# Adding the experts' rows to their tokens for two experts at a time, on one Trainium2 core

## The reference, cut to what matters

```python
combine = jnp.sum(jax.nn.one_hot(eid, N_EXPERTS, dtype=jnp.float32) * (g1 * g2)[..., None], axis=1)
acc = jnp.zeros_like(t)
for e in range(N_EXPERTS):
    hid = jax.nn.silu(t @ w_gate[e].astype(t.dtype)) * (t @ w_up[e].astype(t.dtype))
    acc = acc + combine[:, e:e + 1] * (hid @ w_down[e].astype(t.dtype))
```

## Time and profile before

| | us |
|---|---|
| median of 3 runs | 864.66 (863.48 to 866.47) |
| the profiled execution | 863.17 |
| its span in the trace | 861.4 |
| PE busy | 815.5 (95%) |
| DVE, ACT, POOL busy | 300.6, 120.7, 153.4 |
| mean granted clock of PE | 0.981 of full speed |

### The profile page before, as it was taken

One profiled execution on the slowest core, in us unless ns is written; L12 is line 12 of the kernel. 1 busy time (PEld: TensorE's weight loads), 2 busy tenths in 40 slices (PEclk: granted clock), 3 DMA queues, 4 the chain that ended last, 5 costly groups with the idle time before them and its releaser, 6 DMA issues.

```text
span 861.4 us, 9535 instructions
## 1 busy us (share of the span) xinstructions
PE 815.5 (95%) x3852; PEld 399.6 (46%) x3852; DVE 300.6 (35%) x660; ACT 120.7 (14%) x252; POOL 153.4 (18%) x184
## 2 busy tenths in 40 slices
PE   4999999989899999499999999999999999999994
PEld 3777677768643335433434334343433334343431
DVE  2069999973653613411111111111111111111114
ACT  3211121333431002200000000000000000000002
POOL 2079897600002000110000000000000000000000
PEclk9999999999999999599999999999999999999998
DMA  9893200034235498559999999999999999999921
GB/s 271 310 349 109 98 19 0 8 99 151 70 134 167 134 364 367 237 225 407 423 418 427 402 420 415 406 416 411 422 391 410 406 419 423 413 421 410 428 117 62
DMA packets 50699, 249.37 MB, mean 289 GB/s; under 512 B 7110, under 2 KB 24550, under 8 KB 38351
## 3 DMA queue, kind: packets, MB, share of 16 engines
q1 hardware_dynamic: 44580, 242.75, 71.6%
q10 hardware_dynamic: 3291, 3.20, 1.2%
q0 software_dynamic: 2784, 2.80, 1.2%
HBM read 246.60 MB, written 8.61 MB: 296 GB/s over the span
## 4 chain that ended last, share of the span: by engine, by line
PE 92%; DVE 4%; ACT 2%; issue 1%; DMA 1%; ACTq 0%; POOLq 0%; DVEq 0%
PE bank L1077 26%; PE bank L722 19%; PE bank L1089 13%; PE bank L1100 11%; PE bank L974 8%; PE bank L1067 3%; PE bank L1083 2%; PE bank L804 1%; PE bank L947 1%; PE bank L963 1%; PE bank L938 1%; DVE region_a L1419 1%; PE bank L911 1%; PE bank L881 0%; DVE region_a L1606 0%
## 5 line engine op out<-in xcount | busy, mean ns | idle before, releaser
L722 PE MATMUL bank<-region_a,ring 128*128 128x320 f32 x576 | 158.6, 436 | 0.5 <-DVE region_a L1419 0.5
L722 PEld LDWEIGHTS bank<-region_a,ring 128*128 128x128 f32 x576 | 109.8, 192 | 46.5 <-issue 1.9
L1089 PE MATMUL bank<-ring,vy 128*64 128x512 f32 x512 | 116.9, 598 | 0.0
L1419 DVE TENSOR_TENSOR zz<-zz,bank 64x512 f32<-64x512 f32 x32 | 22.1, 689 | 243.1 <-ACT zz L1380 243.1
L671 POOL DMA_INDIRECT vy<-hn_scratch,region_a x32 | 29.8, 931 | 416.3 <-PE bank L1067 384.1
L1420 DVE SCALAR_TENSOR_TENSOR bank<-region_a,par,bank 128x256 f32<-128x256 f32 x232 | 91.2, 484 | 0.0
L1754 DVE TENSOR_SCALAR vy<-bank,region_a 128x512 f32<-128x512 f32 x32 | 24.0, 751 | 160.2 <-PE bank L1089 160.2
L1078 PE MATMUL bank<-ring,xcx 128*64 128x512 f32 x176 | 79.3, 604 | 0.0
L1078 PE MATMUL bank<-ring,vy 128*64 128x512 f32 x176 | 77.9, 595 | 0.0
L974 PE MATMUL bank<-ring,vy 128*128 128x512 f32 (+1 forms) x192 | 75.6, 606 | 0.0
L1089 PEld LDWEIGHTS bank<-ring,vy 128*64 128x64 f32 x512 | 33.9, 136 | 80.0 <-issue 80.0
(11 more groups left out here) (306 smaller groups left out, 942.4 us busy)
## 6 DMA issues: line engine op xcount, KB each, us to landing
ring<-in_expert_w_down SPq DMA_DIRECT2D x32, 2048.0 KB, 20.7
ring<-in_expert_w_up SPq DMA_DIRECT2D x22, 2048.0 KB, 22.5
region_b<-in_expert_w_gate SPq DMA_DIRECT2D x11, 2048.0 KB, 17.4
ring<-in_expert_w_gate SPq DMA_DIRECT2D x10, 2048.0 KB, 19.1
region_a<-in_expert_w_gate SPq DMA_DIRECT2D x10, 2048.0 KB, 17.7
xcx<-in_expert_w_up SPq DMA_DIRECT2D x10, 2048.0 KB, 22.9
ring<-in_w_in SPq DMA_DIRECT2D x9, 2048.0 KB, 20.0
ring<-in_w_out SPq DMA_DIRECT2D x4, 2048.0 KB, 9.0
```

The source lines that it names most:

```text
L722: ins = pe.matmul(pt[0:m, 0:T], w[:, k, :], ht[:, k, :], start=k == 0, stop=k == KD - 1)
L1089: ins = pe.matmul(b_dn[CAP * q:CAP * q + CAP, :], hidt[b][:, k, :], wd[:, D * k + 512 * q:D * k + 512 * q + 512], start=k == 0, stop=k == 3)
L1419: tt_ = lambda out, a, b, op: dve.tensor_tensor(out, a, b, op)
```

## The change

The addition to the tokens is done for two experts together. Expert 2i's output rows go to partitions 0 to 63 of one buffer `yo` of 1024 columns, those of expert 2i + 1 to partitions 64 to 127; `back` likewise has the slots of both, so `to_tokens` contracts over all 128 rows. The weight moves into the one-hot operand: DVE's `places` compares and multiplies in one instruction, from two new tables `pair_tok` and `pair_w` that are filled behind the slots' tables. ACT instead of DVE copies the output rows from PSUM (`rows_back`), in two halves, unweighted.

```diff
+                k = rows.shape[0]
+                for r, (t0, n) in enumerate(TILES):
+                    for q in range(2):
+                        dst = acc[2 * r + q][:, :] if r < 2 else acc[4][TS * q:TS * q + TS, :]
+                        ins = pe.matmul(dst, rows[:, t0:t0 + n], of[q][0:k, :], start=first, stop=end)
+                    if end:
+                        ins.then_inc(S("summed"), 1)
                 return ins
...
-            def combine(e):
-                pe.wait_ge(S("yo"), e + 1)
-                for r in range(3):
-                    ins = to_tokens(e % 2, r, first=e == 0)
-                ins.then_inc(S("added"), 1)
+            yo_of = [yo[:, 512 * q:512 * q + 512] for q in range(2)]
+
+            def combine(i):
+                pe.wait_ge(S("places"), i + 1)
+                pe.wait_ge(S("yo"), 2 * i + 2)
+                to_tokens(back[i % 2], yo_of, first=i == 0).then_inc(S("added"), 1)
...
-                if e >= 2:
-                    combine(e - 2)
+                if e >= 3 and e % 2:
+                    combine((e - 3) // 2)
...
-            combine(NE - 2)
...
+            pe.wait_ge(S("places"), NE // 2)
             pe.wait_ge(S("yo"), NE)
-            for r in range(3):
-                to_tokens(1, r, end=True).then_inc(S("summed"), 1)
+            to_tokens(back[1], yo_of, end=True)
...
+            def rows_back(e):
+                act.wait_ge(S("dn_done"), e + 1)
+                for q in range(2):
+                    ins = act.activation(yo[CAP * (e % 2):CAP * (e % 2) + CAP, 512 * q:512 * q + 512],
+                                         b_dn[CAP * q:CAP * q + CAP, :], ACT.Copy)
+                ins.then_inc(S("yo"), 1)
+
             for e in range(NE):
...
                 act.activation(sil[b], b_gu[0:CAP, :], ACT.Silu).then_inc(S("sil"), 1)
+                if e:
+                    rows_back(e - 1)
                 act.wait_ge(S("hid_T"), e + 1)
...
+            def pair_values(pt):
+                for j in range(2):
+                    rows = slice(CAP * j, CAP * j + CAP)
+                    dve.tensor_scalar(pair_tok[rows, :], pt[rows, j:NE:2], BIG, None, ALU.add)
+                    ins = dve.tensor_copy(pair_w[rows, :], pt[rows, NE + j:2 * NE:2])
+                return ins
...
-            def weigh(e):
-                b = e % 2
-                wait(dve, S("added"), e - 1)
-                places(b, slice(e, e + 1)).then_inc(S("places"), 1)
-                dve.wait_ge(S("dn_done"), e + 1)
-                dve.wait_ge(S("places"), e + 1)
-                dve.tensor_scalar(yo[b], b_dn[:, :], wsl[:, e:e + 1], None, ALU.mult).then_inc(S("yo"), 1)
+            def places(b, tok, w):
+                return dve.tensor_scalar(back[b], tokno, tok, w, ALU.is_equal, ALU.mult)
...
-                if e:
-                    weigh(e - 1)
-            weigh(NE - 1)
+                if e % 2 == 0:
+                    i = e // 2
+                    wait(dve, S("added"), i - 1)
+                    places(i % 2, pair_tok[:, i:i + 1], pair_w[:, i:i + 1]).then_inc(S("places"), 1)
```

More of the change, by code:

```diff
@@ L280, in build @@
         hid = [zf[0:CAP, 1024 + 512 * b:1536 + 512 * b] for b in range(2)]
-        yo = [vy[:, 512 * b:512 * b + 512] for b in range(2)]
+        yo = vy[:, 0:D]
+        yo_more = [sil[1], hid[1]]
         wr = zf[:, 2048:2048 + KD * 36].rearrange("p (k n) -> p k n", k=KD)
@@ L307, in build @@
         gtok = moe(NE + 1)
+        pair_tok, pair_w = moe(NE // 2), moe(NE // 2)
         gcur = [moe(1).bitcast(I32) for _ in range(2)]
@@ L1091, in down, with to_tokens @@
                 return ins
[L1093 to L1101, removed]
-                return ins
-            def combine(e):
-                pe.wait_ge(S("yo"), e + 1)
-                for r in range(3):
-                    ins = to_tokens(e % 2, r, first=e == 0)
-                ins.then_inc(S("added"), 1)
+            def to_tokens(rows, of, first=False, end=False):
+                k = rows.shape[0]
[5 more added lines that the diff above has]
+                        ins.then_inc(S("summed"), 1)
+                return ins
+            yo_of = [yo[:, 512 * q:512 * q + 512] for q in range(2)]
[3 more added lines that the diff above has]
+                to_tokens(back[i % 2], yo_of, first=i == 0).then_inc(S("added"), 1)
             pe.wait_ge(S("gath0"), 16)
@@ L1158, in _ @@
                         wait_apart(pe, S("sl_y"), n + 1)
-                        for r in range(3):
-                            ins = to_tokens(0, r)
-                        ins.then_inc(S("sl_back"), 1)
+                        to_tokens(back[0][0:CAP, :], yo_more).then_inc(S("sl_back"), 1)
+            pe.wait_ge(S("places"), NE // 2)
             pe.wait_ge(S("yo"), NE)
-            for r in range(3):
-                to_tokens(1, r, end=True).then_inc(S("summed"), 1)
+            to_tokens(back[1], yo_of, end=True)
         @block.scalar
@@ L1387, in _ @@
                         .then_inc(S("gfin_in"), 16)
+            rows_back(NE - 1)
             over = act.value_load(mcount[0:1, 0:1], min_val=0, max_val=T)
@@ L1731, in slot_indices @@
                 return dve.tensor_copy(wsl[:, 0:NE], pt[:, NE:2 * NE])
-            slot_indices(got(dve, "slots")).then_inc(free["dve"], 1)
+            def pair_values(pt):
[4 more added lines that the diff above has]
+                return ins
+            slot_indices(got(dve, "slots"))
+            pair_values(got(dve, "slots")).then_inc(free["dve"], 1)
             after_read(dve, "slots")
@@ L1764, in _ @@
                     tokens(1 - b).then_inc(S("xgt"), 1)
-                if e:
-                    weigh(e - 1)
-            weigh(NE - 1)
+                if e % 2 == 0:
+                    i = e // 2
+                    wait(dve, S("added"), i - 1)
+                    places(i % 2, pair_tok[:, i:i + 1], pair_w[:, i:i + 1]).then_inc(S("places"), 1)
             over = dve.value_load(mcount[0:1, 0:1], min_val=0, max_val=T)
             with dve.If(over > CAP):
-                dve.wait_ge(S("added"), NE - 1)
+                dve.wait_ge(S("added"), NE // 2 - 1)
                 with dve.Fori(0, MAXPASS - 1) as q:
@@ L1785, in _ @@
                         tt_(hid[0], sil[0], b_gu[CAP:P, :], ALU.mult).then_inc(S("sl_hid"), 1)
-                        places(0, bass.ds(e, 1)).then_inc(S("sl_places"), 1)
+                        places(0, gtok[:, bass.ds(e, 1)], wsl[:, bass.ds(e, 1)]).then_inc(S("sl_places"), 1)
                         dve.wait_ge(S("sl_places"), n + 1)
                         dve.wait_ge(S("sl_dn"), n + 1)
-                        dve.tensor_scalar(yo[0], b_dn[:, :], wsl[:, bass.ds(e, 1)], None, ALU.mult)\
-                            .then_inc(S("sl_y"), 1)
+                        for q in range(2):
+                            ins = dve.tensor_copy(yo_more[q], b_dn[CAP * q:CAP * q + CAP, :])
+                        ins.then_inc(S("sl_y"), 1)
             def add_experts(r):
```

2 lines of the change are left out of this document (removed).

## The result

The changed kernel takes 859.49 us (median of 7 runs, 857.7 to 860.7), the kernel before 864.66 on the same chip (now the median of 7 runs too, 861.8 to 866.5); the ratio is 0.994, interval 0.9921 to 0.9959. So it is faster by 0.4 to 0.8%, and the forecast of 858.0 was 1.5 us too low. The profiled execution took 859.03 us, its span is 857.3 where it was 861.4.

What follows compares the result with a forecast made beforehand. PE was taken as the bound, with weight loads only 7.2 us ahead of it; -7.2 (loads) + 0.4 (head) + 1.0 (end) = -5.8 from 863.17 us gave 857.4, set at 858.0 (chance 0.72), range 850 to 864.

Steps and rivals of the forecast that it cites:

- a pair of experts on PE: Expert loop on PE, before any waits for loads: two experts take 29.00 us instead of 30.06.
- addition of two experts: Expert loop on PE: adding two experts' rows to the tokens with 128 rows takes 4.5 to 4.7 us.
- PE's own saving up to gate/up 31: Expert loop: PE alone would reach gate/up of expert 31 17.6 us earlier.
- PE's time lost to them: Late expert loop, from about expert 20: PE waits for weight loads, some 10 us in total.
- last up load lands: End of the expert loads: the up weights of expert 31 still land near 818 us.
- let through by the loads: Start of gate/up of expert 31: the weight loads allow a gain of 7.2 us instead of 17.6.
- head: Before the expert loop: four more small DVE operations cost 0.4 us, bounds 0.3 to 0.8.
- end of the loop: From gate/up of expert 31 to DVE's first addition to xt: 24.1 us instead of 23.13, +1.0.
- R1: Expert loop: loads go faster when asked, PE stays the bound, all 17.6 us come, 847.0 us; chance 0.10.
- R2: Expert loop: no gain, through slower loads or slower 128-row matmuls, about 864 us; chance 0.12.
- R3: Expert loop: more loads in flight share the engines and delay the needed one, slower, 867.8 us; chance 0.06.
- R4: Expert loop: PE's pauses of about 1 us an expert lower its clock; given nothing of its own, left inside R2.

Runs made afterwards that it cites:

- e2: The changed kernel with only half of each down unit loaded (wrong weights in the other half): 848.68 us, ratio 0.9840 to the kernel before.
- e4: The changed kernel with eight weight slots instead of nine: 862.04 us, ratio 0.9991 to the kernel before.
- e3: The kernel before with eight weight slots instead of nine: 863.58 us, ratio 1.0007.
- e1: The kernel before with only half of each down unit loaded (stale weights in the other half): 863.96 us, ratio 1.0011.
- e12: e7 with the four table operations moved behind the release of the gather: 856.77 us, ratio 0.9917 to the kernel before.
- e5: The changed kernel run once more, unaltered: 856.62 us, ratio 0.9908 to the kernel before.
- e8: The changed kernel with the edits of e6 and e7 together: 853.92 us, ratio 0.9879 to the kernel before.
- e10: The changed kernel, but DVE instead of ACT copies each expert's output rows: 857.61 us, ratio 0.9928 to the kernel before.
- e7: The changed kernel; last down product in gate/up's bank, ACT copies hidden rows first, DVE half the last rows: 857.98 us, ratio 0.9930 to the kernel before.
- e6: The changed kernel with ten idle products on PE ahead of the first gate/up: 855.19 us, ratio 0.9902 to the kernel before.
- e11: The kernel before with ten idle products on PE ahead of the first gate/up: 862.81 us, ratio 0.9992.

## Why the prediction was right, point by point

The step that carried it, that the weight loads would take over from PE and let only their lead of 7.2 us through, is shown from three sides: PE's starts at the landings, e2 (fewer bytes give the rest back), and e4 beside e3 (a slot fewer costs time only where PE is no longer the bound).

| step | forecast | measured |
|---|---|---|
| a pair of experts on PE | 29.00 us | 28.99 |
| addition of two experts | 4.5 to 4.7 | 4.54 |
| PE's own saving up to gate/up 31 | 17.6 | 17.68 (e1, e2) |
| first wait for a load | near expert 20 | expert 20 (21 in five other traces) |
| PE's time lost to them | some 10 | 7.0 of waits, 3.4 of half clock |
| longest delay of an up load | towards 38 | 38.8 |
| last up load lands | near 818 | 819.9 |
| let through by the loads | 7.2 | 6.93 |
| head | +0.4 | +1.3 |
| end of the loop | +1.0 | +0.9 |
| time against its own profiled execution | -5.8 | -4.1 |

That 7.2 and 6.93 agree so closely is luck in part. In the seven traces of changed kernels with full loads and nine slots the loop is 450.80 less 4.98 to 8.95 us, with 6.93 in the middle; the mechanism is borne out by all of them, the last 2 us by none. The last up load is 2 us later than forecast because the whole loop starts 1.87 later (376.13 against 374.26); its landing is read from PE's start at 820.00.

The last line adds up: -6.93 + 1.33 + 0.92 is -4.68, and 0.54 comes from ahead of the slots (360.33 against 359.79), where nothing was changed and where other traces of the two kernels begin anywhere from 357.8 to 360.5.

*The term that was mis-sized* is the head, priced at 0.4 with a bound of 0.8. The four operations cost what was said: from DVE's first slot operation to PE's first transpose it takes 4.46 us instead of 4.00. Missed was the first gate/up: it takes 9.35 us instead of 8.49, because more of it runs at half clock. 0.46 and 0.86 are the 1.3. In e12, with the operations moved, both are gone (3.94 and 8.57). Since the loads of the loop wait for the end of that product, all of it reaches the end.

*R1* (loads go faster when asked) is refuted: 414 GB/s after, 415 before, with a queue 8 us deeper. The ceiling of 435 GB/s that the Trainium skill gives (DMA: Bandwidth & Descriptors, Where 436 GB/s comes from) lies above both and isn't contradicted by them; my working took a ceiling for a rate that can be had. Nor does 415 contradict the 358 GB/s of the same page, as I had written: its section on bandwidth gives this as the share of each core when both cores of a pair stream.

*R2* wasn't the case, but its mechanism is real: with loads as the bound the loop is 441.85 to 445.82 us in the seven traces, where PE as the bound gives 450.80 to 450.82 in five. Not all of that spread is the pace of the loads. The three longest loops (e5, e8 and e10, 444.44 to 445.82) are those in which the second gate/up took 8.4 to 8.6 us instead of 7.02, partly at half clock, so that the loop's next loads were asked for 1.5 to 1.6 us later. The forecast's own range for this, 6.5 us down and 4 up, was wider than what came.

*R3* didn't show: gate and up of expert 29, issued within 0.4 us, landed 32.6 and 37.1 us later, at 785.1 and 790.0, one after the other.

*R4* was right in its weight and wrong in its reason. I had written that pauses of this size don't bring the clock down. The pauses come bunched, not 1 us at each expert, and those of 3.2 and 1.9 us were followed by half clock. The first line is PE from 668.50 to 671.80, with the granted clock third from the right. Behind the wait at 668.28 the pairs of records start 0.85 us apart and then 0.43 again:

```profile
668.50:671.80 3.30, 3.30 (x10) 1.17 (x8) 0.00 (x0) 0.00 (x0) 0.00 (x0) 0.50 0.98 412
...
668.98 1.06 PE L1079 MATMUL bank<-region_a,vy 128*64 128x512 f32 x1
669.84 1.06 PE L1079 MATMUL bank<-region_a,vy 128*64 128x512 f32 x1
...
672.15 0.59 PE L1079 MATMUL bank<-region_a,vy 128*64 128x512 f32 x1
672.58 0.59 PE L1079 MATMUL bank<-region_a,vy 128*64 128x512 f32 x1
```

That gate/up lasts 8.72 us (668.28 to 677.00), the one at 759.54 8.71, the last 7.02. Two times 1.7 us, 10.4 with the 7.0 of waiting: about the 10.75 that PE lost to the loads (17.68 - 6.93). In this trace the half clock delayed nothing at the end: the last gate/up starts 0.1 us after its load. In e10 it was paid. Gate/up of expert 29 took 8.71 us there (791.07), and that of expert 31 started at 821.75, 1.4 us after its load had landed (784.12 + 36.2 = 820.3):

```profile
784.12 0.43 SPq L446 DMA_DIRECT2D ring<-in_expert_w_up  x1
...
ring<-in_expert_w_up SPq DMA_DIRECT2D x1, 2048.0 KB, 36.2
...
821.75 0.64 PE L1079 MATMUL bank<-region_b,vy 128*64 128x512 f32 x1
```

The length of the pause alone doesn't decide it. e7 had three of 1.8 to 1.9 us (at 666.24, 697.14 and 757.85), and its clock stayed full:

```profile
PE bank L1079 <- issue: 8.3, 6, 1.9
...
660.00:820.00 160.00, 151.70 (x692) 61.12 (x693) 17.12 (x28) 23.12 (x43) 8.33 (x9) 1.00 1.01 418
```

The rule that 64 rows can run two at a time (TensorEngine Tiling (Array Packing) of the Trainium skill) agrees with the trace here: filling the array's rows saved 2 slots in 12, not half. Two slots of 0.43 are 0.86 of the 1.07 us by which a pair of experts got shorter.

## What to carry to other kernels

When the queue of loads is always full and the delay from issue to landing grows from one turn of the loop to the next, the loop is living on its buffers. What a faster compute engine can gain is then about the lead that is left at the last turn (last use minus last landing), whatever it saves itself; the rest turns into waiting. Here that lead was 7 us of the 17.7 that PE saved, and single executions gave 5 to 9. And an operation ahead of the first product of such a loop is paid in full, with what goes with it in the clock of the start: 0.45 us of work came to 1.1 or more.

## What the runs showed of the hardware that was not expected

- PE as the bound repeats to 0.02 us over 450 us in five traces; the loads as the bound spread over 4.0 us in seven, part of it through PE's clock.
- Idle products don't bring the clock back reliably: with PE busy from 358.75 it was back near 363 (e6), from 360.75 near 365.5 (e8), from 360.63 near 369 (e11). Only the first two gained from them.
- A pause of 1.9 us on PE was already followed, 1 us into the next product, by records at half pace (759.54 in the changed kernel), while three of 1.8 to 1.9 us in e7 were not. Every trace has a pause of 1.2 us shortly before the second gate/up; in e5, e8 and e10 half clock followed, in the other eleven it didn't.
